# Gate/up products of a decoder layer: two matmuls instead of three, whole PSUM banks, copies on ScalarE, an accumulating DMA

## The chip, the cores and the metric

The kernel runs on one core of one Trainium2 chip. The metric is the device time of a run in microseconds (us); lower is better. Three runs of the kernel before gave 2072.7 us as median (2071.96 to 2073.09).

## What is computed

One layer of a decoder with 512 positions and model width 2048, everything in float32: a norm, an input projection, two kinds of windowed attention, an output projection, and then the feed-forward part that this document is about. Cut to that part, the reference reads:

```python
h = rmsnorm(x, ffn_norm[l])
gate = jnp.einsum('bsd,df->bsf', h, w_gate[l])     # 512 x 2048 by 2048 x 5632
up = jnp.einsum('bsd,df->bsf', h, w_up[l])         # the same shape
x = x + jnp.einsum('bsf,fd->bsd', jax.nn.silu(gate) * up, w_down[l])
```

## The kernel before

**Precision.** A float32 product is made out of the faster fp32r type. Each operand is split into a high part (a copy rounded to fp32r) and a low part (what is left), and three matmuls are added into PSUM: high times high, high times low, low times high. The function `three` (lines 437 to 441) issues them.

**Seven products instead of eight.** Gate and up form a block product of 2 by 2 blocks: two blocks of weights by two blocks of the 512 positions, over pairs of depth blocks. The kernel uses a fast scheme of Strassen's kind: seven products of sums of blocks, each with 128 weight columns and 256 positions (`HALF`), stand for eight plain ones. The sums of the position blocks are made once (`s_hi`, `s_lo`, seven slots of 256 for each of eight pairs). The sums of the weight blocks are made for each tile of weights.

**Groups and doubles.** The 5632 columns of gate and up are 44 groups (`TILES`) of 128 columns. A group goes over the depth in four steps, called doubles, so there are 176. In a double, the queue of SyncE (SP) loads the gate and the up weights (two DMAs, line 355) into one of three buffers `t_raw`; VectorE (DVE) makes the sums (`t_sums`, lines 1467 and 1470); ScalarE (ACT) makes the high parts (`t_high`, line 1012: 128x1792); VectorE makes the low parts (`t_low`, line 1476); TensorE (PE) runs `double` (lines 516 to 528): two depth blocks, seven products, three matmuls each with 256 moving columns, 42 in all. The step `t_high` of a double waits until TensorE is done with the double three before it, since there are three buffers.

**PSUM.** The seven 256-wide results share four banks (`PRODUCTS`, line 70), and groups alternate between two sets of four banks, so that a group accumulates while the one before it is read.

**After a group.** `cross` (lines 1015 to 1022) copies three of the results to SBUF on ScalarE. `post_first` and `post_second` (lines 1480 to 1497) combine the seven results into gate and up with four VectorE instructions that read PSUM. `store_gu` (lines 357 to 361) on SP's queue writes the 512 KB tile to DRAM (`gu_mid`), from two alternating buffers.

**Order.** Each engine's order is written out by hand. In `six_groups` VectorE runs `t_sums(j)`, then `t_low(j - 1)`; the combining of the group before comes in behind the latter where j % 4 is 3 (first half) and in the next step (second half). ScalarE runs `t_high(j)`, then `cross` where j % 4 is 2. GpSimd (POOL) does nothing in this stage but one small power.

**The next stage** is the down projection: 44 tiles of activation are loaded back, silu and the product are made, each is split into high and low (`down_high`, `down_low`), and TensorE runs units of twelve 512-wide matmuls (`down_unit`, lines 530 to 545, `wide_products`, lines 477 to 482).

Of the kernel before, what the change touches and what calls it, by code (L numbers as in the profile page):

```python
# [9 lines left out]
F32R = mybir.dt.float32r  # L10
# [60 lines left out]
BOTH, CROSS, OTHER, SPREAD = 0, 1, 2, 3  # L71
SPREAD_T = 27
# [15 lines left out]
def build(nc, x, attn_norm, w_in, sinks, out_norm_a, out_norm_b, w_out, ffn_norm,  # L88
# [90 lines left out]
    s_hi = [sb(f"s_hi{j}", [P, QUAD, HALF], F32R, at=places_s[j]) for j in range(KD // 2)]  # L179
    s_lo = [sb(f"s_lo{j}", [P, QUAD, HALF], F32R, at=places_s[j] + S_SIZE) for j in range(KD // 2)]  # L180
# [7 lines left out]
    gu_out = [sb(f"gu_out{r}", [P, 4, HALF], at=place_ez + 4096 * r) for r in range(2)]  # L188
    crossed = sb("crossed", [P, 3, HALF], at=place_ez + 8192)
    junk = sb("junk", [P, SEQ], at=place_ez + 9216)  # L190
    r2_bc = sb("r2_bc", [P, SEQ], at=place_x)
    r2_wide = sb("r2_wide", [P, NT, P], at=place_x + 6144)

    places_u = [place_x + 2048, place_raw0, place_raw0 + 4096, place_raw1, place_raw1 + 4096,
# [44 lines left out]
    crossed_done, post_done = sem("crossed_done"), sem("post_done")  # L239
    gu_stored = [sem(f"gu_stored{r}") for r in range(2)]  # L240
# [73 lines left out]
    def _(sp):  # L314
# [42 lines left out]
        def store_gu(i, gj):  # L357

            dst = gu_mid[bass.ds(LOOP_G * i + gj, 1), :, :].rearrange("o p c -> p (o c)")
            sp.wait_ge(post_done, 4 * (LOOP_G * i + gj) + 4)  # L360
            sp.dma_start(dst, gu_out[gj % 2][:, :, :].rearrange("p a c -> p (a c)")).then_inc(gu_stored[gj % 2], 16)

# [5 lines left out]
        with sp.Fori(0, 7) as i:  # L368
            for j in range(8, 32):
                load_double(i, j)  # L370
                if j % 4 == 2:
                    store_gu(i, j // 4 - 2)

        def load_gu(i, k):

            src = gu_mid[bass.ds(8 * i + k, 1), :, :].rearrange("o p c -> p (o c)")
            if isinstance(i, int) and i < 2:
                sp.wait_ge(gu_stored[k % 2], 16 * (4 * i + k // 2 + 1))
# [8 lines left out]

        load_gu(0, 0)
# [9 lines left out]
        store_gu(7, 0)  # L398
        for s in range(4, 32):
# [9 lines left out]
            if s == 15:  # L409
                store_gu(7, 1)  # L410
            if 16 <= s < 24:
                load_gu(1, s - 16)
        for r in range(2):
            sp.wait_ge(gu_stored[r], 16 * TILES // 2)
# [21 lines left out]
    def _(pe):  # L436
# [79 lines left out]
        def double(j):  # L516
# [3 lines left out]
            for q in range(2):  # L520
                sh, sl = s_hi[2 * d + q], s_lo[2 * d + q]
                for ti, si, which, h in PRODUCTS:
                    b = bank[BANK_SET[gj % 2][which]][:, HALF * h:HALF * (h + 1)]
                    if j == SPREAD_T + 1 and q == 0 and which == SPREAD:
                        pe.wait_ge(rbc_done, 2)
                    mm = three(b, t_hi[r][:, ti, q, :], t_lo[r][:, ti, q, :], sh[:, si, :], sl[:, si, :],
                               d == 0 and q == 0 and h == 0, d == DOUBLES - 1 and q == 1)
            mm.then_inc(t_used, 1)

        def down_unit(i, s):  # L530
# [6 lines left out]
            for t in range(NT):  # L537
                if k == 0 and isinstance(i, int) and i == 0 and n < 2:
                    pe.wait_ge(post_done, 4 * (TILES - 1 + n))
                elif k == 0:  # L540
                    pe.wait_ge(grp_taken, 4 * group + t - 7)
# [200 lines left out]
        for j in range(ALL_T):  # L742
# [5 lines left out]
            if g >= 2 and d == 0:  # L748
                pe.wait_ge(post_done, 4 * (g - 1))
            double(j)  # L750
            if j == 0:
                turn_mix(NC - 1)
            if j == SPREAD_T:
                pe.wait_ge(post_done, 4 * g)
                spread_r(r2_wide, 2, BANK_SET[(g + 1) % 2][SPREAD])
# [28 lines left out]
    def _(act):  # L784
# [230 lines left out]
        def cross(i, gj):  # L1015

            b = half_banks(gj, CROSS)
            act.wait_ge(t_used, used_by(i, gj))
            if not (isinstance(i, int) and i == 0 and gj == 0):
                act.wait_ge(post_done, 4 * (LOOP_G * i + gj) - 2)  # L1020
            nc.scalar.activation(crossed[:, 0:2, :], b, ACT.Copy).then_inc(crossed_done, 1)
            nc.scalar.activation(crossed[:, 2, :], b[:, 0, :], ACT.Copy).then_inc(crossed_done, 1)
# [785 lines left out]
```

## Time and profile before

| | |
|---|---|
| median of three runs | 2072.7 us |
| the profiled execution | 2072.31 us |
| its span, first to last instruction | 2070.5 us |
| granted TensorE clock, mean | 0.998 of full speed |
| TensorE (PE) busy | 2046.9 us (99%) |
| VectorE (DVE) busy | 1448.5 us (70%) |
| ScalarE (ACT) busy | 874.2 us (42%) |
| GpSimd (POOL) busy | 117.9 us (6%) |

The profile is of one execution. Matmuls are pipelined and the end of each is modelled, so the duration of a matmul says less than the distance from one start to the next. Busy time of an engine that waits for another is no cost; a wait matters where it sits on the chain that ends last.

### The profile page before, as it was taken

The page shows a single profiled execution, that of the slowest core. Times are in us where ns is not written, and L with a number is a line of the kernel's source. Part 1 is how long each engine was busy: PE and PEld are TensorE (multiplying, and loading weights), DVE is VectorE, ACT ScalarE, POOL GpSimd, SP SyncE. Part 2 cuts the span into 40 slices and gives each one's busy share as a digit, 9 for nine tenths or more (in the row PEclk, how much of TensorE's full clock was granted, in tenths as well). Part 3 has the DMA queues.
Part 4 walks back from the last instruction along what each step waited for, and adds up shares of the span by engine and source line. Part 5 has one row for each costly group of instructions (what it writes and reads, how often), then busy time and mean ns, then how long its engine had stood idle before and what let it go on. Part 6 is the DMA issues. An engine that isn't in the chain of part 4 may idle for free.

```text
span 2070.5 us, 35030 instructions
## 1 busy us (share of the span) xinstructions
PE 2046.9 (99%) x12886; PEld 1851.5 (89%) x12886; DVE 1448.5 (70%) x2174; ACT 874.2 (42%) x1381; POOL 117.9 (6%) x191
## 2 busy tenths in 40 slices
PE   8999999999999899999999999999999999999998
PEld 7888888887888899999999999999999888888886
DVE  5466666666666898787878888787887646545446
ACT  5455556555436533333333333333334333333333
POOL 0022222222100000000000000000000000000000
PEclk9999999999999999999999999999999999999999
DMA  6322222224334344444444444444447763654533
GB/s 188 92 71 78 72 73 73 72 71 152 78 99 139 112 143 126 138 132 126 134 131 134 123 136 133 129 133 129 136 123 233 249 178 97 177 138 136 137 96 132
DMA packets 317391, 261.41 MB, mean 126 GB/s; under 512 B 13872, under 2 KB 268128, under 8 KB 316768
## 3 DMA queue, kind: packets, MB, share of 16 engines
q1 hardware_dynamic: 309840, 248.11, 40.6%
q10 hardware_dynamic: 7440, 11.72, 1.6%
q8 instruction: 83, 1.36, 0.3%
q14 instruction: 28, 0.23, 0.0%
HBM read 228.31 MB, written 31.46 MB: 125 GB/s over the span
## 4 chain that ended last, share of the span: by engine, by line
PE 82%; DVE 6%; issue 5%; ACT 5%; DMA 1%; SPq 0%; ACTq 0%; DVEq 0%; POOLq 0%; POOL 0%
PE bank L439 18%; PE bank L441 18%; PE bank L440 18%; PE bank L480 9%; PE bank L482 9%; PE bank L481 9%; ACT probs L833 1%; PE bank L569 1%; ACT w_hi L790 1%; DVE w_lo L1195 1%; ACT s_raw L999 1%; DVE s_lo L1460 1%; PE bank L586 1%; PE bank L585 1%; ACT s_hi L982 1%
## 5 line engine op out<-in xcount | busy, mean ns | idle before, releaser
L439 PE MATMUL bank<-s_hi,t_hi 128*128 128x256 f32 x2464 | 698.5, 283 | 5.7 <-DVE t_lo L1476 5.7
L440 PE MATMUL bank<-s_lo,t_hi 128*128 128x256 f32 x2464 | 698.0, 283 | 0.0
L441 PE MATMUL bank<-s_hi,t_lo 128*128 128x256 f32 x2464 | 697.9, 283 | 0.0
L1012 ACT ACTIVATE t_hi<-t_raw 128x1792 fp32r<-128x1792 f32 x176 | 299.6, 1703 | 536.9 <-PE bank L441 509.0
L1195 DVE TENSOR_TENSOR w_lo<-raw,w_hi 128x512 fp32r<-128x512 f32 x364 | 253.2, 697 | 388.0 <-ACT w_hi L790 385.8
L439 PEld LDWEIGHTS bank<-s_hi,t_hi 128*128 128x128 f32 x2464 | 473.7, 192 | 6.6 <-issue 6.6
L440 PEld LDWEIGHTS bank<-s_lo,t_hi 128*128 128x128 f32 x2464 | 473.8, 192 | 0.0
L441 PEld LDWEIGHTS bank<-s_hi,t_lo 128*128 128x128 f32 x2464 | 473.8, 192 | 0.0
L1476 DVE TENSOR_TENSOR t_lo<-t_raw,t_hi 128x1792 fp32r<-128x1792 f32 x176 | 356.3, 2025 | 145.7 <-ACT t_hi L1012 145.7
L790 ACT ACTIVATE w_hi<-raw 128x512 fp32r<-128x512 f32 x364 | 229.1, 631 | 491.2 <-PE bank L482 355.1
L480 PE MATMUL bank<-w_hi,down_hi 128*128 128x512 f32 x640 | 249.0, 389 | 0.0
L481 PE MATMUL bank<-w_lo,down_hi 128*128 128x512 f32 x640 | 249.0, 389 | 0.0
L482 PE MATMUL bank<-w_hi,down_lo 128*128 128x512 f32 x640 | 249.0, 389 | 0.0
L1467 DVE TENSOR_TENSOR t_raw<-t_raw 128x1024 f32<-128x1024 f32 x176 | 214.3, 1217 | 7.0 <-DMA t_raw<-in_w_up 6.9
L439 PE MATMUL bank<-h_hi,w_hi 128*128 128x512 f32 x544 | 218.6, 402 | 0.4 <-DVE h_lo L1199 0.4
L441 PE MATMUL bank<-h_hi,w_lo 128*128 128x512 f32 x544 | 212.9, 391 | 0.0
L440 PE MATMUL bank<-h_lo,w_hi 128*128 128x512 f32 x544 | 212.8, 391 | 0.0
L482 PEld LDWEIGHTS bank<-w_hi,down_lo 128*128 128x128 f32 x640 | 120.1, 188 | 25.2
L480 PEld LDWEIGHTS bank<-w_hi,down_hi 128*128 128x128 f32 x640 | 120.1, 188 | 24.8
L481 PEld LDWEIGHTS bank<-w_lo,down_hi 128*128 128x128 f32 x640 | 120.1, 188 | 24.8
L441 PEld LDWEIGHTS bank<-h_hi,w_lo 128*128 128x128 f32 x544 | 102.1, 188 | 22.5
L439 PEld LDWEIGHTS bank<-h_hi,w_hi 128*128 128x128 f32 x544 | 102.4, 188 | 19.5 <-DVE h_lo L1199 0.8
(162 smaller groups left out, 2280.9 us busy)
## 6 DMA issues: line engine op xcount, KB each, us to landing
raw<-in_w_down SPq DMA_DIRECT2D x176, 256.0 KB, 2.9
t_raw<-in_w_gate SPq DMA_DIRECT2D x174, 256.0 KB, 3.1
t_raw<-in_w_up SPq DMA_DIRECT2D x174, 256.0 KB, 3.4
raw<-in_w_in SPq DMA_DIRECT2D x136, 256.0 KB, 2.9
gu_mid<-gu_out SPq DMA_DIRECT2D x44, 512.0 KB, 3.8
gu_s<-gu_mid SPq DMA_DIRECT2D x44, 512.0 KB, 5.1
raw<-in_w_out SPq DMA_DIRECT2D x64, 256.0 KB, 2.9
x_first<-in_x SPq DMA_DIRECT2D x8, 512.0 KB, 7.4
```

Of the source, the lines that this page charges most:

```text
L439: nc.tensor.matmul(out_ap, st_hi, mv_hi, start=start, stop=False, skip_group_check=True)
L440: nc.tensor.matmul(out_ap, st_hi, mv_lo, start=False, stop=False, skip_group_check=True)
L441: return nc.tensor.matmul(out_ap, st_lo, mv_hi, start=False, stop=stop, skip_group_check=True)
L480: nc.tensor.matmul(b[:, :], ah[:, ts], w_hi[:, slot, :], start=first, stop=False, skip_group_check=True)
L481: nc.tensor.matmul(b[:, :], ah[:, ts], w_lo[:, slot, :], start=False, stop=False, skip_group_check=True)
L482: return nc.tensor.matmul(b[:, :], al[:, ts], w_hi[:, slot, :], start=False, stop=last, skip_group_check=True)
L569: mm = nc.tensor.transpose(bank[BANK_PT][:, c0 + P * n:c0 + P * (n + 1)], probs[h % 2][:, e:e + P], ident[:, :])
L790: nc.scalar.activation(w_hi[:, s, :], raw[:, s, :], ACT.Copy).then_inc(w_hi_done, 1)
L1012: nc.scalar.activation(t_hi[r][:, :, :, :].rearrange("p a q c -> p (a q c)"), t_raw[r][:, 1:8, :, :].rearrange("p a q c -> p (a q c)"), AC ...
L1195: nc.vector.tensor_tensor(w_lo[:, s, :], raw[:, s, :], w_hi[:, s, :].bitcast(F32), ALU.subtract).then_inc(w_lo_done, 1)
L1467: nc.vector.tensor_tensor(x[:, 2:6, :].rearrange("p (a b) c -> p a b c", b=2), x[:, 0:9:8, :].unsqueeze(2).broadcast_to([P, 2, 2, HALF]), ...
L1476: nc.vector.tensor_tensor(t_lo[r][:, :, :, :].rearrange("p a q c -> p (a q c)"), t_raw[r][:, 1:8, :, :].rearrange("p a q c -> p (a q c)"), ...
```

## The change

For the groups from the third on (42 of 44):

- **Matmuls.** The high and low parts of the position sums become one tile (`s_two`, 2 by 7 by 256). High weights by both halves is one matmul of 512 moving columns; low weights by the high half is a second of 256. Two matmuls stand where three stood; the number of moving columns stays 768.
- **PSUM.** Each product takes a bank of its own (columns 0 to 255: the high positions; 256 to 511: the low positions). Seven banks are in use, and every group uses the same seven. The first double of a group waits, product by product, for the bank to have been copied out.
- **Copies.** ScalarE copies both halves of each of the seven banks to SBUF, 14 copies of 128x256 a group: the low halves into `part_low`, the high ones into `part`. It does so ahead of `t_high` where j % 4 is 2, and product by product as TensorE finishes them. There is one buffer of each.
- **Adding the halves.** GpSimd's queue issues a DMA (`fold`) from `part_low` to `part`, both in SBUF, 128 x 7168 bytes (896 KB), with add as accumulate operation.
- **Combining.** `post` on VectorE has five instructions, all on SBUF, in one place (behind `t_low(j - 1)` where j % 4 is 3), and first waits for the fold. The store to DRAM is issued by GpSimd's queue and waits for `post`. The next group's copies wait for the fold and `post` of the group before, and from the fourth product on for its store.
- The first two groups keep the three matmuls, but are copied out by ScalarE with four copies each (`take_halves`) and combined by `post`. Some small tiles move, and the last group's copies stand ahead of the second tile's high part in the down stage.

The core of the diff (places of tiles and the down stage are left out):

```diff
+SEVEN = [(0, 4, 4), (6, 3, 5), (5, 2, 6), (2, 5, 1), (3, 1, 2), (1, 6, 0), (4, 0, 3)]
+SEVEN_BANK = (0, 4, 6, 1, 2, 3, 5)
...
+    def taken_by(i, gj):
+
+        g = LOOP_G * i + gj
+        return 4 * (g + 1) if isinstance(g, int) and g < 2 else 14 * g - 6
...
+        def double_wide(j):
+
+            r, (g, d) = j % RING_T, (j // DOUBLES, j % DOUBLES)
+            pe.wait_ge(t_lo_done, j + 1)
+            for i, (ti, si, _) in enumerate(SEVEN):
+                b = bank[SEVEN_BANK[i]]
+                if d == 0 and g == 2:
+                    pe.wait_ge(bank_taken, 4 if i < 4 else i + 1)
+                elif d == 0:
+                    pe.wait_ge(bank_taken, taken_by(0, g - 2) + 2 * (i + 1))
+                for q in range(2):
+                    both = s_two[2 * d + q][:, :, si, :]
+                    nc.tensor.matmul(b[:, :].rearrange("p (a c) -> p a c", c=HALF), t_hi[r][:, ti, q, :], both,
+                                     start=d == 0 and q == 0, stop=False, skip_group_check=True)
+                    mm = nc.tensor.matmul(b[:, 0:HALF], t_lo[r][:, ti, q, :], both[:, 0, :], start=False,
+                                          stop=d == DOUBLES - 1 and q == 1, skip_group_check=True)
+                if d == DOUBLES - 1 and i < QUAD - 1:
+                    mm.then_inc(prod_ready, 1)
             mm.then_inc(t_used, 1)
...
+        def take_products(i, gj, i0=0, i1=QUAD):
+
+            g = LOOP_G * i + gj
+            for p in range(i0, i1):
+                b, slot = bank[SEVEN_BANK[p]], SEVEN[p][2]
+                if p == 0:
+                    slots_free(i, gj, False)
...
+                        act.wait_ge(folded, 16 * (g - 2))
+                if p == 3:
+                    slots_free(i, gj, True)
+                if p < QUAD - 1:
+                    act.wait_ge(prod_ready, (QUAD - 1) * (g - 2) + p + 1)
+                else:
+                    act.wait_ge(t_used, used_by(i, gj))
+                nc.scalar.activation(part_low[:, slot, :], b[:, HALF:2 * HALF], ACT.Copy).then_inc(bank_taken, 1)
+                nc.scalar.activation(part[:, slot, :], b[:, 0:HALF], ACT.Copy).then_inc(bank_taken, 1)
...
+                if j % 4 == 2 and not (first and j == 10):
+                    take_products(i, j // 4 - 1)
                 t_high(i, j)
                 if first and j == 8:
-                    cross(0, 0)
-                if j % 4 == 2:
-                    cross(i, j // 4 - 1)
+                    take_halves(0)
+                if first and j == 10:
+                    take_halves(1)
...
+        def post(i, gj):
+
+            g = LOOP_G * i + gj
+            if isinstance(g, int) and g < 2:
+                dve.wait_ge(bank_taken, taken_by(i, gj))
+            else:
+                dve.wait_ge(folded, 16 * (g - 1))
+            nc.vector.tensor_tensor(part[:, 1, :], part[:, 1, :], part[:, 5, :], ALU.add).then_inc(post_done, 1)
+            nc.vector.tensor_tensor(part[:, 2, :], part[:, 2, :], part[:, 4, :], ALU.add).then_inc(post_done, 1)
+            dve.wait_ge(post_done, POSTS * g + 2)
+            nc.vector.tensor_tensor(part[:, 1:3, :], part[:, 1:3, :], part[:, 0:4:3, :], ALU.add).then_inc(post_done, 1)
+            dve.wait_ge(post_done, POSTS * g + 3)
+            nc.vector.tensor_tensor(part[:, 1:3, :], part[:, 1:3, :], part[:, 6:7, :].broadcast_to([P, 2, HALF]), ALU.add).then_inc(post_done, 1)
+            nc.vector.tensor_tensor(part[:, 0:4:3, :], part[:, 0:4:3, :], part[:, 4:6, :], ALU.subtract).then_inc(post_done, 1)
...
                 if first and j == 8:
-                    post_first(0, 0)
-                if j % 4 == 0:
-                    post_second(i, j // 4 - 2)
+                    post(0, 0)
                 if j % 4 == 3:
-                    post_first(i, j // 4 - 1)
+                    post(i, j // 4 - 1)
...
+        def store_gu(g):
+
+            pool.wait_ge(post_done, POSTS * (g + 1))
+            nc.gpsimd.dma_start(gu_mid[g, :, :], part[:, 0:4, :].rearrange("p a c -> p (a c)")).then_inc(gu_stored, 16)
+
+        def fold(g):
+
+            pool.wait_ge(bank_taken, taken_by(0, g))
+            nc.gpsimd.dma_start(part[:, :, :].rearrange("p a c -> p (a c)"), part_low[:, :, :].rearrange("p a c -> p (a c)"),
+                                accum_op=ALU.add).then_inc(folded, 16)
+
+        for g in range(TILES):
+            if g >= 2:
+                fold(g)
+            store_gu(g)
```

## Rows read from the trace of the kernel before

**Rows 1.** The page: busy time of each engine, and the chain that ended last.

```profile
PE 2046.9 (99%) x12886; PEld 1851.5 (89%) x12886; DVE 1448.5 (70%) x2174; ACT 874.2 (42%) x1381; POOL 117.9 (6%) x191
PE 82%; DVE 6%; issue 5%; ACT 5%; DMA 1%; SPq 0%; ACTq 0%; DVEq 0%; POOLq 0%; POOL 0%
```

**Rows 2.** Stretches: busy us of PE, PEld, DVE, ACT, POOL; clock, DMA share, GB/s.

```profile
600.00:700.00 100.00, 96.21 (x478) 81.78 (x477) 64.75 (x82) 53.26 (x97) 0.00 (x0) 0.98 0.45 130
...
770.00:1400.00 630.00, 630.00 (x5253) 630.00 (x5252) 514.57 (x506) 236.84 (x188) 0.00 (x0) 1.00 0.43 131
```

**Rows 3.** Timeline of PE, gate/up stage: start us, duration us, engine, line, operation.

```profile
1199.78 0.28 PE L439 MATMUL bank<-s_hi,t_hi 128*128 128x256 f32 x1
1199.90 0.28 PE L440 MATMUL bank<-s_lo,t_hi 128*128 128x256 f32 x1
...
1201.94 0.28 PE L439 MATMUL bank<-s_hi,t_hi 128*128 128x256 f32 x1
```

**Rows 4.** Timeline of PE, down stage.

```profile
1700.21 0.39 PE L480 MATMUL bank<-w_hi,down_hi 128*128 128x512 f32 x1
...
1701.57 0.39 PE L480 MATMUL bank<-w_hi,down_hi 128*128 128x512 f32 x1
```

**Rows 5.** Timeline of ACT, gate/up stage; in brackets the idle time before, and its releaser.

```profile
1201.12 1.70 ACT L1012 ACTIVATE t_hi<-t_raw 128x1792 fp32r<-128x1792 f32 x1 [3.34 <-PE bank L441]
1202.73 0.57 ACT L1021 ACTIVATE crossed<-bank 128x512 f32<-128x512 f32 x1
1203.20 0.38 ACT L1022 ACTIVATE crossed<-bank 128x256 f32<-128x256 f32 x1
```

**Rows 6.** Timeline of DVE, gate/up stage: first its third group, then the middle.

```profile
749.45 1.21 DVE L1467 TENSOR_TENSOR t_raw<-t_raw 128x1024 f32<-128x1024 f32 x1
750.58 0.42 DVE L1470 TENSOR_TENSOR t_raw<-t_raw 128x256 f32<-128x256 f32 x1
750.92 2.02 DVE L1476 TENSOR_TENSOR t_lo<-t_raw,t_hi 128x1792 fp32r<-128x1792 f32 x1
752.85 1.22 DVE L1467 TENSOR_TENSOR t_raw<-t_raw 128x1024 f32<-128x1024 f32 x1
...
1202.86 2.02 DVE L1476 TENSOR_TENSOR t_lo<-t_raw,t_hi 128x1792 fp32r<-128x1792 f32 x1 [1.54 <-ACT t_hi L1012]
1204.80 0.68 DVE L1487 TENSOR_TENSOR gu_out<-bank,crossed 128x512 f32<-128x512 f32 x1
1205.40 0.68 DVE L1488 TENSOR_TENSOR gu_out<-bank,crossed 128x512 f32<-128x512 f32 x1
...
1209.84 0.69 DVE L1494 TENSOR_TENSOR gu_out<-bank,gu_out 128x512 f32<-128x512 f32 x1
1210.56 0.69 DVE L1496 TENSOR_TENSOR gu_out<-bank,gu_out 128x512 f32<-128x512 f32 x1
```

**Rows 7.** Waits in the stage, 740 to 1605 us: us in total, times, longest us.

```profile
ACT t_hi L1012 <- PE bank L441: 509.0, 162, 3.4
DVE t_lo L1476 <- ACT t_hi L1012: 143.3, 158, 2.9
```

**Rows 8.** DMA issues: out<-in, queue, count, KB each, median us to landing.

```profile
t_raw<-in_w_up SPq DMA_DIRECT2D x174, 256.0 KB, 3.4
gu_mid<-gu_out SPq DMA_DIRECT2D x44, 512.0 KB, 3.8
x_mix<-in_x ACTq DMA_DIRECT2D x4, 1024.0 KB, 10.3
x_mid<-x_mix ACTq DMA_DIRECT2D x4, 1024.0 KB, 4.5
out_x<-x_res SPq DMA_DIRECT2D x3, 1024.0 KB, 3.8
out_x<-x_res SPq DMA_DIRECT2D x1, 512.0 KB, 2.6
```

**Rows 9.** Start of the stage: PE's third group begins; ACT and DVE before it.

```profile
736.22 0.36 PE L439 MATMUL bank<-s_hi,t_hi 128*128 128x256 f32 x1 [0.23 <-DVE t_lo L1476]
...
728.99 0.58 ACT L1021 ACTIVATE crossed<-bank 128x512 f32<-128x512 f32 x1
...
729.93 0.69 DVE L1487 TENSOR_TENSOR gu_out<-bank,crossed 128x512 f32<-128x512 f32 x1 [0.66 <-ACT crossed L1022]
```

**Rows 10.** End of the stage: DVE's second low part; PE's first 512-wide matmuls of the down stage.

```profile
1581.53 0.68 DVE L1204 TENSOR_TENSOR down_lo<-gu_s,down_hi 128x512 fp32r<-128x512 f32 x1
...
L480 PE MATMUL bank<-w_hi,down_hi x24: 389/389/396, 1583.9 to 1599.6; 128*128 128x512 f32 x24
```

More of the change, by code:

```diff
@@ L187, in build @@
     t_lo = [sb(f"t_lo{r}", [P, QUAD, 2, P], F32R, at=places_t[r] + S_SIZE) for r in range(RING_T)]
-    gu_out = [sb(f"gu_out{r}", [P, 4, HALF], at=place_ez + 4096 * r) for r in range(2)]
-    crossed = sb("crossed", [P, 3, HALF], at=place_ez + 8192)
+    part = sb("part", [P, QUAD, HALF], at=place_ez)
+    part_low = sb("part_low", [P, QUAD, HALF], at=place_x)
     junk = sb("junk", [P, SEQ], at=place_ez + 9216)
-    r2_bc = sb("r2_bc", [P, SEQ], at=place_x)
-    r2_wide = sb("r2_wide", [P, NT, P], at=place_x + 6144)
-    places_u = [place_x + 2048, place_raw0, place_raw0 + 4096, place_raw1, place_raw1 + 4096,
+    junk_last = sb("junk_last", [P, SEQ], at=place_x)
+    r2_bc = sb("r2_bc", [P, SEQ], at=place_g + 14336)
+    r2_wide = sb("r2_wide", [P, NT, P], at=place_ez + 7168)
+    places_u = [place_ez + 7168, place_raw0, place_raw0 + 4096, place_raw1, place_raw1 + 4096,
                 place_t1, place_t1 + 4096, place_t1 + 8192]
@@ L747, in _ @@
                 pe.wait_ge(s_raw_done, 40)
-            if g >= 2 and d == 0:
-                pe.wait_ge(post_done, 4 * (g - 1))
-            double(j)
+            if g < 2:
+                double(j)
+            else:
+                double_wide(j)
             if j == 0:
@@ L1013, in t_high, with slots_free, take_halves @@
                                  t_raw[r][:, 1:8, :, :].rearrange("p a q c -> p (a q c)"), ACT.Copy).then_inc(t_hi_done, 1)
[L1015 to L1022, printed above, removed]
+        def slots_free(i, gj, stored_too):
+            g = LOOP_G * i + gj
+            act.wait_ge(post_done, POSTS * g)
+            if stored_too:
+                act.wait_ge(gu_stored, 16 * g)
+        def take_halves(gj):
+            act.wait_ge(t_used, used_by(0, gj))
+            if gj == 0:
+                act.wait_ge(s_sum_done, 3 * 8)
+            else:
+                slots_free(0, gj, True)
+            for which, slots in ((BOTH, slice(0, 4, 3)), (CROSS, slice(4, 6)), (OTHER, slice(1, 3)), (SPREAD, slice(6, 7))):
+                b = half_banks(gj, which)
+                if which == SPREAD:
+                    b = b[:, 0:1, :]
+                nc.scalar.activation(part[:, slots, :], b, ACT.Copy).then_inc(bank_taken, 1)
+        def take_products(i, gj, i0=0, i1=QUAD):
[4 more added lines that the diff above has]
+                    slots_free(i, gj, False)
+                    if isinstance(g, int) and g == 2:
+                        act.wait_ge(x_spilled[NC - 1], 16)
+                        act.wait_ge(sq_done, FIRST_SQ + 16)
+                    else:
+                        act.wait_ge(folded, 16 * (g - 2))
[3 more added lines that the diff above has]
+                    act.wait_ge(prod_ready, (QUAD - 1) * (g - 2) + p + 1)
+                else:
+                    act.wait_ge(t_used, used_by(i, gj))
+                nc.scalar.activation(part_low[:, slot, :], b[:, HALF:2 * HALF], ACT.Copy).then_inc(bank_taken, 1)
+                nc.scalar.activation(part[:, slot, :], b[:, 0:HALF], ACT.Copy).then_inc(bank_taken, 1)
         act.wait_ge(kb_lo_done, 4)
@@ L1138, in down @@
                     silu(0, s + 4)
-                if first and s == 6:
-                    cross(7, 1)
                 if 13 <= s < 13 + next_tiles:
@@ L1635, in down @@
                 if first and s == 6:
-                    post_first(7, 1)
-                    post_second(7, 1)
+                    post(7, 1)
                 if s % 8 < 2:
@@ L1649, in down @@
                     down_low(i + 1, s - 25)
-        for k in range(2):
-            gate_scaled(0, k)
+        gate_scaled(0, 0)
         gate_times_up(0, 0)
```

85 lines of the change are left out of this document (34 added, 51 removed).

## The prediction

> **What bounds the kernel now.** I read the page first: TensorE is busy for 99% of the span and makes up 82% of the chain that ended last [rows 1]. Then the stretch of the gate/up stage, from 770 us on: in 630 us TensorE never pauses, at full clock, while VectorE works 514.6 us, ScalarE 236.8 us, GpSimd nothing, and the DMA engines 43% [rows 2]. Then the starts of its matmuls. From 1199.78 to 1201.94 us there are 18 steps of 0.120 us [rows 3], for 256 columns each. In the down stage 6 steps of 512 columns take 1.36 us, 0.2267 us each [rows 4]. The difference, 256 columns in 0.1067 us, is 2.4 GHz exactly. So each matmul costs 0.1067 us per 256 columns **and a further 0.0133 us**, whether it is wide or narrow. A double of 42 narrow matmuls takes 5.04 us, a group of four 20.15 us.
>
> Last I read who waits. ScalarE's high parts wait for TensorE to free a buffer (509 us in all) and VectorE's low parts for ScalarE (143 us) [rows 7]. Both engines run ahead: at 1201.12 ScalarE begins the high parts of a double, VectorE has the low ones at 1204.8 [rows 5, 6], and TensorE wants them two doubles (10.1 us) after the buffer came free. About 6 us of slack.
>
> **The matmuls.** In 42 groups x 4 doubles x 14 triples = 2352 places, three matmuls (0.360 us) become one of 512 and one of 256: 0.2267 + 0.120 = 0.3467 us. That is 0.0133 us each, 31 us in all; a group falls from 20.15 to 19.41 us. No row has a 512-wide matmul whose moving columns lie in two pieces; from below I bound it by the row of a contiguous one (no cost), from above by two narrow ones, which would give back all 31 us. The row it is nearest to is the contiguous one; I take that. If two pieces cost as much as two matmuls, nothing is gained.
>
> The Trainium skill, "TensorE: Matmul & The Clock Gate", section "Wait — 56ns, not 53.3ns?", gives about 2.5 ns as the fixed cost of a warm matmul. By it the change would be worth 6 us. Rows 3 and 4 show 13.3 ns for this kernel's fp32r matmuls, and the sum goes by them.
>
> **ScalarE.** Out go two copies a group (0.57 and 0.38 us), in come 14 of 128x256. Back to back a copy costs its duration less 0.10 us (1202.73 to 1203.20 for one of 0.57) [rows 5], so 0.28 us, 3.9 us a group. With four high parts at 1.61 us that is 10.3 us of 19.4: room enough. They are hidden in part by the last double of a group: ScalarE is free 2.1 us into it, TensorE finishes a product every 0.69 us and the copies need 0.56, so they end about 1.1 us after the group. The first double of the next group asks for its banks in the same order, 0.69 us apart from the group's end on; the bank asked for last is wanted 4.2 us after it. Cost of the seven banks: nothing, 3 us of cover.
>
> **VectorE.** A double is 1.47 us of sums and 1.93 us of low parts, start to start [rows 6]. Four instructions of 2.6 us a group go. The five of post: two of 256 wide (0.36 and 0.48), one of 512 behind a wait (0.75), two more of 0.60 to 0.65 (from the distances 0.60 and 0.72 in rows 6): 2.8 us. Together 16.4 of 19.4 us. Enough, if VectorE isn't made to wait.
>
> **SP's queue** loses 44 issues of stores; nothing waits for them. GpSimd's queue gets 44 stores and 42 folds and has nothing else. Its store is needed only at the fourth product of the next group's copies; 3.8 us [rows 8] or twice that fits.
>
> **The fold and what is queued behind it** decide the case. Post waits in order on VectorE until the fold has landed, and behind post stand the sums of one double and the low parts of another that TensorE needs. Call L the time from the last copy to the moment VectorE sees the fold. If the fold is late, the group becomes a loop: post 2.8, sums 1.47, low 1.93, sums of the next double 1.47 (0.1 to be seen), high parts 1.61, 14 copies 3.86 (0.15 to be seen), and L again: **13.4 + L**. Up to L = 6.0 us TensorE's 19.41 stays the longer; at L = 6.7 the group is as long as before; from there each us of L costs 42 us.
>
> No row has an accumulating DMA or one issued by GpSimd. Bounds: from below the 1024 KB store without other traffic, 3.8 us; from above the 1024 KB load beside other traffic, 10.3 us. The nearest row is the store of 1024 KB from SBUF beside weight loads, 4.5 us [rows 8]: nearly the same size, the same source, and a DMA share of 0.45 around it against 0.43 in the stage [rows 2]. For issue by software and the second operand I add 1 us, an estimate between the ends: L = 5.5. So the fold stays hidden, with half a us of cover only.
>
> **Ends of the stage.** At its start there is no slack: TensorE waits 0.23 us for low parts at 736.22 [rows 9]. VectorE's combining waits for ScalarE there, whose copies of the first group now take 1.9 us instead of 0.9, +1.1 us; the second group's copies stand behind a high part, and the new group's fifth product waits for them, some 0.8 us. I take 2 us (0 to 5). At the end, the second tile's low part was ready at 1582.2, 4 us before it was wanted [rows 10]; the first unit begins at about 1583.5 and has 12 matmuls of 0.2267 us. The last group's copies now stand ahead of it; by the same chain it comes 0.4 us before it is wanted. I take 0.5 us (0 to 3).
>
> **Sum**, against the profiled execution's own 2072.3 us (the median of the runs is 2072.7, 0.4 above it): -31.0 + 2.0 + 0.5 = **2043.8 us**.
>
> **Rivals.**
> (a) *The accumulating DMA moves its data at half speed.* It must read part_low and part and write part. By rows 8, 512 and 1024 KB without traffic take 2.6 and 3.8 us: 1.2 us for 512 KB over a fixed 1.4. A second read of 896 KB adds 2.1 us to the 4.5 of the nearest row: L = 6.6, group 20.0 us, time 2072.3 - 42 x 0.15 + 2.5 = 2068.5. The stage's own stores speak for traffic that counts (3.8 us against 2.6).
> The Trainium skill, "Collectives: The Full Stack", section "The bandwidth ceiling: the fold count and why AG ≠ RS ≠ AR", states such a rule: an add in the DMA path needs two reads that share one ring, and so runs at about half the rate of a copy. No row here can show it.
> (b) *Slower.* The same, plus 1 us or so for GpSimd's issue and the second read stretched by the weight loads, which arrive every 4.9 us: L = 7.5, group 20.9, and the loop through VectorE's queue, not TensorE, sets the pace. 2072.3 + 42 x 0.75 + 2.5 = 2106. With L = 8, 2127; at the upper bound of 10.3, 2224. It decides from L = 6.8 on. For it: the cover is thin, both buffers are single, and no row excludes it. Against it: the store at 4.5 us.
> (c) *The wide matmul in two pieces brings nothing*: 20.15 a group, 2075 at best, about no change.
>
> **Chances.** Forecast (L up to 6.0) 0.43. Partly used up (6.0 to 6.6, the case of (a)) 0.11, 2044 to 2068. Within 0.2%, about 4 us, which is what a measurement of this kernel can tell from no change: 0.06, from (a) at its far end and (c). (b) 0.40. So faster 0.54, same 0.06, slower 0.40. The forecast's own range is 2041 to 2049; since both signs hold much of the chance, the range for 8 in 10 runs from 2040 to L = 8.1, 2130.
>
> **What the profile after would show.** Right: starts of a wide and a narrow matmul 0.347 us apart for the pair; a group of 19.4 us; TensorE without idle time in the stage; VectorE waiting for the fold before post but the low parts still early; fold to landing under 6 us. Wrong: TensorE idle once a group ahead of its fourth double, released by t_lo, and VectorE idle ahead of post, released by the DMA; then L can be read from the landing and the loop's sum checked. If the pair takes 0.36 us, it is (c). If TensorE is idle ahead of a group's first double, the banks are late, which I have priced at nothing.

## The result, and the profile of the kernel after

The change makes the kernel slower. Four runs gave a median of 2152.3 us (2151.9 to 2154.1), against 2072.9 us for four runs of the kernel before: a ratio of 1.0385, interval 1.0371 to 1.0400, or 79.5 us. The profiled execution took 2152.76 us, its span 2150.8 us, at a mean clock of 0.989.

The page: busy time, then the chain that ended last, by engine and by line.

```profile
PE 2053.3 (95%) x10534; PEld 1737.2 (81%) x10534; DVE 1449.9 (67%) x2218; ACT 1004.7 (47%) x1889; POOL 178.9 (8%) x277
...
PE 47%; DVE 17%; DMA 16%; issue 9%; ACT 9%; ACTq 0%; SPq 0%; DVEq 0%; POOL 0%; POOLq 0%
DMA part<-part_low 16%; PE bank L480 9%; PE bank L482 9%; PE bank L481 9%; DVE t_lo L1530 4%; PE bank L439 4%; PE bank L441 4%; PE bank L440 4%; PE bank L540 4%; DVE t_raw L1521 3%; ACT part L1075 3%; ACT part_low L1074 2%; PE bank L542 2%; DVE part L1544 1%; ACT w_hi L811 1%
```

Against [rows 1] TensorE's share of the chain falls from 82% to 47%, and one DMA, the fold, holds 16%. A share like that for a transfer that was to be hidden is the first thing to see. There are 2352 matmuls fewer, as written, so the change does what it says.

The same stretch as in [rows 2], and the four us of it in which the clock was low:

```profile
770.00:1400.00 630.00, 581.57 (x3207) 499.57 (x3206) 475.59 (x496) 305.46 (x522) 39.84 (x57) 0.98 0.62 161
1196.00:1200.00 4.00, 4.00 (x17) 3.44 (x17) 3.35 (x4) 2.80 (x6) 0.00 (x0) 0.64 0.44 131
```

TensorE now stands still for 48 of 630 us, where it never paused before. VectorE's busy time in the whole span didn't grow (1449.9 against 1448.5 us; the 630 us hold fewer groups now), nor is any other engine near its limit. So nothing is too busy: something is waited for in turn. The waits of 700 to 1700 us say what (line, releaser: us in total, times, longest):

```profile
ACT t_hi L1033 <- DVE t_raw L1524: 383.7, 89, 8.7
DVE part L1541 <- DMA part<-part_low: 179.9, 41, 6.7
ACT t_hi L1033 <- PE bank L542: 88.1, 40, 8.1
...
PE bank L540 <- DVE t_lo L1530: 67.2, 42, 2.7
DVE t_raw L1521 <- DMA t_raw<-in_w_up: 40.3, 47, 1.9
...
PE bank L540 <- ACT part L1075: 1.3, 1, 1.3
```

Read them from the bottom up. The banks, which I had priced at nothing, cost 1.3 us once. TensorE waits once a group for low parts, 67 us in all. ScalarE's high parts used to wait for TensorE [rows 7]; now they wait for VectorE's sums. And VectorE waits 4.4 us in each group, at the first instruction of `post`, for the fold. The DMA issues (KB each, median us from issue to landing) give its length, against a neighbour and the store:

```profile
t_raw<-in_w_up SPq DMA_DIRECT2D x174, 256.0 KB, 4.0
part<-part_low POOLq DMA_DIRECT2D x42, 896.0 KB, 8.1
gu_mid<-part POOLq DMA_DIRECT2D x44, 512.0 KB, 2.9
```

One turn of the loop, from the timelines of VectorE, ScalarE, GpSimd and TensorE (start us, duration, what it is, idle time before and its releaser):

```profile
1211.52 0.43 DVE L1541 TENSOR_TENSOR part<-part 128x256 f32<-128x256 f32 x1 [4.70 <-DMA part<-part_low]
...
1213.65 0.68 DVE L1547 TENSOR_TENSOR part<-part 128x512 f32<-128x512 f32 x1
1214.25 1.22 DVE L1521 TENSOR_TENSOR t_raw<-t_raw 128x1024 f32<-128x1024 f32 x1
...
1215.72 2.02 DVE L1530 TENSOR_TENSOR t_lo<-t_raw,t_hi 128x1792 fp32r<-128x1792 f32 x1
1217.66 1.22 DVE L1521 TENSOR_TENSOR t_raw<-t_raw 128x1024 f32<-128x1024 f32 x1
...
1217.79 0.50 PE L540 MATMUL bank<-s_two,t_hi 128*128 128x512 f32 x1 [0.48 <-DVE t_lo L1530]
...
1219.24 1.71 ACT L1033 ACTIVATE t_hi<-t_raw 128x1792 fp32r<-128x1792 f32 x1 [1.70 <-DVE t_raw L1524]
...
1224.27 0.54 ACT L1075 ACTIVATE part<-bank 128x256 f32<-128x256 f32 x1
...
1225.11 0.85 POOL L1817 DMA_DIRECT2D part<-part_low  x1 [9.93 <-ACT part L1075]
...
1232.91 0.42 DVE L1541 TENSOR_TENSOR part<-part 128x256 f32<-128x256 f32 x1 [3.72 <-DMA part<-part_low]
```

From `post` to `post` 21.39 us: 13.29 us until the last copy ends at 1224.81 (post, sums, low parts, sums, high parts, 14 copies, the loop of the prediction), and 8.10 us more until VectorE sees the fold. TensorE isn't in this loop at all; it is fed late by it. Over 40 such turns in the timeline, the loop without the fold has a median of 13.30 us, and L, the time from the last copy to the first instruction of `post`, a median of 8.4 and a mean of 8.45.

**The sum of the slowdown.** The mean over the 40 groups is 22.01 us against 20.15 before: 74.4 us. Of it (13.30 + 8.45 - 20.15) x 40 = 64 us are the loop, and 10 us are excesses over 13.30, nearly all in eleven groups, which the last section takes up under the clock. The remaining 6 us of the difference of the two spans (80.3) lie at the ends of the stage.

### The profile page after: what moved, and what is told of

It is laid out like the page before. It is cut to its first block, busy times and chain, and to the rows that moved or that the text cites. A ratio compares the mean times of both kernels' runs of the same rounds, so it can differ in the third digit from the quotient of the medians.

```text
span 2150.8 us, 31007 instructions
## 1 busy us (share of the span) xinstructions
PE 2053.3 (95%) x10534; PEld 1737.2 (81%) x10534; DVE 1449.9 (67%) x2218; ACT 1004.7 (47%) x1889; POOL 178.9 (8%) x277
## 4 chain that ended last, share of the span: by engine, by line
PE 47%; DVE 17%; DMA 16%; issue 9%; ACT 9%; ACTq 0%; SPq 0%; DVEq 0%; POOL 0%; POOLq 0%
DMA part<-part_low 16%; PE bank L480 9%; PE bank L482 9%; PE bank L481 9%; DVE t_lo L1530 4%; PE bank L439 4%; PE bank L441 4%; PE bank L440 4%; PE bank L540 4%; DVE t_raw L1521 3%; ACT part L1075 3%; ACT part_low L1074 2%; PE bank L542 2%; DVE part L1544 1%; ACT w_hi L811 1%
## 5 line engine op out<-in xcount | busy, mean ns | idle before, releaser
L540 PE MATMUL bank<-s_two,t_hi 128*128 128x512 f32 x2352 | 847.6, 404 | 69.1 <-DVE t_lo L1530 67.2
L542 PE MATMUL bank<-s_two,t_lo 128*128 128x256 f32 x2352 | 666.5, 283 | 0.0
L540 PEld LDWEIGHTS bank<-s_two,t_hi 128*128 128x128 f32 x2352 | 450.2, 191 | 189.1 <-DVE t_lo L1530 81.9
L1033 ACT ACTIVATE t_hi<-t_raw 128x1792 fp32r<-128x1792 f32 x176 | 304.0, 1728 | 482.0 <-DVE t_raw L1524 393.8
L542 PEld LDWEIGHTS bank<-s_two,t_lo 128*128 128x128 f32 x2352 | 452.8, 193 | 0.0
L1521 DVE TENSOR_TENSOR t_raw<-t_raw 128x1024 f32<-128x1024 f32 x176 | 214.8, 1220 | 40.5 <-DMA t_raw<-in_w_up 40.3
L1541 DVE TENSOR_TENSOR part<-part 128x256 f32<-128x256 f32 x44 | 18.7, 425 | 181.5 <-DMA part<-part_low 179.9
L1075 ACT ACTIVATE part<-bank 128x256 f32<-128x256 f32 x294 | 128.7, 438 | 0.0
L1074 ACT ACTIVATE part_low<-bank 128x256 f32<-128x256 f32 x294 | 125.6, 427 | 1.9 <-PE bank L542 1.0
```

The costliest lines, as they stand in the source:

```text
L540: nc.tensor.matmul(b[:, :].rearrange("p (a c) -> p a c", c=HALF), t_hi[r][:, ti, q, :], both, start=d == 0 and q == 0, stop=False, skip_gr ...
L542: mm = nc.tensor.matmul(b[:, 0:HALF], t_lo[r][:, ti, q, :], both[:, 0, :], start=False, stop=d == DOUBLES - 1 and q == 1, skip_group_check ...
L1033: nc.scalar.activation(t_hi[r][:, :, :, :].rearrange("p a q c -> p (a q c)"), t_raw[r][:, 1:8, :, :].rearrange("p a q c -> p (a q c)"), AC ...
L1521: nc.vector.tensor_tensor(x[:, 2:6, :].rearrange("p (a b) c -> p a b c", b=2), x[:, 0:9:8, :].unsqueeze(2).broadcast_to([P, 2, 2, HALF]), ...
```

## Experiments

The first three kernels below and the one without a fold were run once each, the others four to ten times. Each is compared with the kernel before, run beside it. Two explanations were to be told apart at first: that the adding in the DMA makes it slow, or that the transfer as such, its issue by GpSimd or its company of weight loads, does. And one question stood beside them: does anything but the fold cost time?

**The fold as a plain copy.** All else is kept, the same bytes go to the same place, but they overwrite the high halves there: the two halves aren't added.

```diff
-            nc.gpsimd.dma_start(part[...], part_low[...], accum_op=ALU.add).then_inc(folded, 16)
+            nc.gpsimd.dma_start(part[...], part_low[...]).then_inc(folded, 16)
```

> The fold is a plain copy from part_low to part (no adding, so the two halves are not added). Theory A (the accumulating DMA moves its packets one by one at less than half the rate of a copy, and that is most of the late fold): by the 4096-byte packets of the store, 896 KB need about 2.3 us of data phase instead of 4.6, the time L from the last copy to the start of post falls from 8.4 to about 6.0 us, the loop through VectorE's queue (13.3 + L) to 19.3 us, so that TensorE's 14 pairs x 4 doubles x 0.350 = 19.6 us is the longer; time about 2055 us. Theory B (issue by GpSimd and the traffic of the weight loads are what makes it late, the adding costs nothing): L stays at 7.5 to 8.4, time 2110 to 2152 us.

Measured: 2059.1 us, beside 2073.1 for the kernel before on that chip. L falls to 5.5 us and the group to 19.8 us. That is more than the loop needs (13.3 + 5.5 = 18.8 us): TensorE sets the pace here, at a distance of its matmuls that the section "VectorE adds, no fold" explains. The DMA view of one fold in each kernel (queue, kind: packets, MB, share of 16 engines; then the issues), first after, in 1225 to 1233 us:

```profile
q0 software_dynamic: 144, 0.92, 71.0%
...
part<-part_low POOLq DMA_DIRECT2D x1, 896.0 KB, 7.8
t_raw<-in_w_gate SPq DMA_DIRECT2D x2, 256.0 KB, 7.0
t_raw<-in_w_up SPq DMA_DIRECT2D x2, 256.0 KB, 7.4
```

and the plain copy, 1211 to 1220 us:

```profile
q0 software_dynamic: 144, 0.92, 24.3%
...
part<-part_low POOLq DMA_DIRECT2D x1, 896.0 KB, 5.7
t_raw<-in_w_gate SPq DMA_DIRECT2D x2, 256.0 KB, 3.1
t_raw<-in_w_up SPq DMA_DIRECT2D x2, 256.0 KB, 3.5
```

The same 0.92 MB occupies the 16 engines for 0.71 x 8 = 5.7 us when it is added, for 0.243 x 9 = 2.2 us when it is copied. Over the whole stage the median packet of 7168 bytes takes 553 ns against 273 ns, and each engine has eight of them. The loads issued beside it land in 7.0 to 7.4 us in place of 3.1 to 3.5. GpSimd also spends 0.86 us on each issue of the adding DMA and 0.53 us on one of the plain. So it is the adding. The Trainium skill, "Collectives: The Full Stack", section "The bandwidth ceiling: the fold count and why AG ≠ RS ≠ AR", gives a reason for a collective that adds (ReduceScatter): two operands are read through one ring, at about half the rate of a copy. The trace agrees with the rate, with a factor of 2.0 for the median packet; that one ring is the cause, no run here shows. The estimate for a plain transfer of this size by the Trainium skill, "DMA: Bandwidth & Descriptors", section "Anatomy of one DMA — SWDGE (gpsimd) path", is about 4.1 us; 5.1 us were measured as the median here, with weight loads on the same engines, and 4.2 us where `post` stands later (below).

**The plain copy issued by ScalarE.** The copy stands in ScalarE's queue behind the last of the fourteen, GpSimd issues only the stores.

```diff
+            if i1 == QUAD:
+                act.wait_ge(bank_taken, taken_by(i, gj))
+                act.dma_start(part[...], part_low[...]).then_inc(folded, 16)
```

> The same plain copy (the halves are not added), issued by ScalarE's queue right behind its last copy instead of by GpSimd. It measures what the issue by GpSimd adds to L. Theory A: about 1 us, L about 5.0, time about 2055 us as in the kernel with the plain copy from GpSimd, since both are below the 6.3 us from which TensorE waits. Theory B: most of L is the issue by GpSimd, so L falls from 7.5 or more to 5 or less and the time from over 2110 to 2055 us.

Measured: 2063.5 us, L 5.5 us, median landing 5.5 us where GpSimd's was 5.1. Issue by GpSimd costs nothing that shows in L, and the us that I had put between the two queues isn't there. The 4.4 us by which this kernel is the slower of the two fit TensorE's matmuls, whose pairs keep the longer of two distances throughout here and in some 60% of the stage there (see "VectorE adds, no fold").

**Three of seven slots added.** The fold moves 384 KB and still adds; the low halves of the other four slots are left out.

```diff
-            nc.gpsimd.dma_start(part[:, :, :]..., part_low[:, :, :]..., accum_op=ALU.add)
+            nc.gpsimd.dma_start(part[:, 4:7, :]..., part_low[:, 4:7, :]..., accum_op=ALU.add)
```

> The accumulating DMA takes three of the seven slots (384 KB instead of 896 KB; the low halves of the other four are not added). Theory A: the data phase is 3/7 of 4.6 us, 2.0 us, so L is about 5.8 us and TensorE doesn't wait; time about 2055 us. Theory B (fixed costs of the software queue): L falls by less than 1 us, time over 2100 us.

Measured: 2050.8 us, L 5.7 us, landing 5.4, a group of 19.44 us. With 3/7 of the bytes L falls by 2.7 of 8.4 us. From these two points I estimate a part of L that goes with bytes, about 2.7 us for 512 KB, and a fixed one of some 3.7 us. Below 6 us it is hidden, as the prediction had it.

**No fold.** The low halves are copied out but never added. `post` waits for the copies in place of the fold, and the next group's copies no longer wait for a fold.

```diff
-                dve.wait_ge(folded, 16 * (g - 1))
+            dve.wait_ge(bank_taken, taken_by(i, gj))
```

> No fold at all (the low halves are copied out but not added); post waits for the copies. It shows what the change gives without its DMA: 31 us less for the matmuls, 3 to 5 us for the two ends of the stage: 2045 to 2049 us, and TensorE's pairs at 0.347 us as in the kernel that adds three slots. If the pairs stay at 0.350 us or the time is over 2060 us, something other than the fold holds the stage up too.

Measured: 2047.0 us beside 2073.8, so 26.8 us faster. The group takes 19.41 us from `post` to `post`, the number of the prediction; past the start of the stage TensorE waits but once, 1.3 us for a bank. Six steps from wide matmul to wide matmul take 2.08 us, 0.3467 each:

```profile
1203.80 0.39 PE L540 MATMUL bank<-s_two,t_hi 128*128 128x512 f32 x1
1204.03 0.28 PE L542 MATMUL bank<-s_two,t_lo 128*128 128x256 f32 x1
...
1205.88 0.39 PE L540 MATMUL bank<-s_two,t_hi 128*128 128x512 f32 x1
```

This settles three points at once: the wide matmul in two pieces costs no more than a contiguous one; seven single banks and 14 copies cost 1.3 us; and all but some 4 us of the 31 arrive. Whatever the change loses, it loses by the fold.

**The fold in two.** Slots 4 to 6, whose banks are copied first, are folded while ScalarE copies the other four.

```diff
+            for taken, slots in ((taken_by(0, g) - 8, slice(4, 7)), (taken_by(0, g), slice(0, 4))):
+                pool.wait_ge(bank_taken, taken)
+                nc.gpsimd.dma_start(part[:, slots, :]..., part_low[:, slots, :]..., accum_op=ALU.add).then_inc(folded, 16)
```

> The fold is two accumulating DMAs: slots 4 to 6 as soon as the first three products are copied out, slots 0 to 3 (512 KB) behind the last copy; post where the changed kernel has it, output the reference's. Theory A: what counts is the data phase of what is left after the last copy, 4/7 of 4.7 us, 2.7 us, so L is 6.0 to 6.4 us instead of 8.4, the loop (13.3 + L) 19.3 to 19.7 us, about TensorE's own 19.5; time 2050 to 2060 us, faster than both kernels. If the two DMAs share the engines so that the first holds up the second, L stays over 7.5 and the time over 2105 us.

Measured: 2080.3 us, ratio 1.0031 (1.0019 to 1.0044): no faster than before. L is 6.7 us, more than expected, and the period 20.07 us. The loop without the fold again takes 13.29 us in the median: the loop's sum holds at a second value of L. The second piece takes 6.4 us for 512 KB, more than the 5.4 that 384 KB took alone.

**`post` one double later.** Nothing is made shorter; `post` goes behind the low parts of the next double, so the fold has one double more before VectorE's queue stands behind it.

```diff
-                if j % 4 == 3:
-                    post(i, j // 4 - 1)
+                if j % 4 == 0:
+                    post(i, j // 4 - 2)
```

> Post stands one step later in VectorE's order, behind the low parts of the next double (where j % 4 is 0), everything else as in the changed kernel, output the reference's. Theory A (the loss is the work queued behind the waiting post): L stays at about 8.4 us, but the low parts that TensorE wants for its fourth double are done before post waits; TensorE doesn't wait, a group takes 14 x 4 x 0.350 = 19.6 us, time 2072.9 - 42 x 0.55 + 5 = about 2055 us (2048 to 2065), and the dips of TensorE's clock go with the pauses. Rival C (the single buffer is the limit: fold, post, store and the next copies one behind another): the copies of the next group wait for the store or for post, time over 2100 us.

Measured: 2060.7 us as the median of ten runs between 2051.3 and 2084.7; the ratio, without the longest, is 0.9933 (0.9909 to 0.9958). In the middle of its runs, moving `post` turns 3.9% slower into 0.7% faster, with a fold about as long as before (7.8 us to landing, against 8.1); only 10 of the 42 `post` behind a fold wait for it. But the runs scatter as those of no other kernel here, and the profiled one took 2080.9 us. In its steady groups the period is 19.79; in others it is 21 to 23. One of these, from the timelines of GpSimd, SP and VectorE:

```profile
903.96 0.86 POOL L1816 DMA_DIRECT2D part<-part_low  x1 [6.52 <-ACT part L1075]
...
904.05 0.86 SPq L366 DMA_DIRECT2D t_raw<-in_w_up  x1
...
912.71 1.23 DVE L1521 TENSOR_TENSOR t_raw<-t_raw 128x1024 f32<-128x1024 f32 x1 [4.84 <-DMA t_raw<-in_w_up]
```

A weight load issued 0.09 us after the fold is seen 8.7 us later, where its median in the kernel after is 4.0. So when VectorE no longer waits for the fold, it may wait for the load that shares the engines with it. In the kernel after, such loads were late too, but VectorE stood still for the fold anyway. The steady 19.79 us aren't 19.41 because of the second distance of the matmuls (see "VectorE adds, no fold"); how much of the scatter comes from it and how much from late loads isn't shown.

**Both: in two, and later.**

> Both: the fold in two, and post one step later in VectorE's order; output the reference's. If the disturbed groups of the kernel with post later (weight loads that land 5 us late while the fold of 896 KB is in flight) come from the long fold, the shorter pieces end them: 2048 to 2056 us with little scatter. If they come from the place of post, the scatter of 2051 to 2085 us stays.

Measured: 2100.8 us, ratio 1.0132 (1.0117 to 1.0148), some 45 us above what was expected. The two edits, each a gain, don't add up. The waits of its stage, 740 to 1605 us:

```profile
DVE t_raw L1521 <- DMA t_raw<-in_w_up: 154.0, 78, 5.2
...
PE bank L540 <- ACT part L1075: 32.3, 29, 1.5
DVE part L1541 <- DMA part<-part_low: 4.5, 2, 3.9
```

The fold is hidden (4.5 us in all), and the loads are late instead (154 us, against 35 after in the same stretch). Which coincidence of loads and folds makes the period 21.0 us was not taken further.

**`post` later, and the plain copy.** The halves aren't added here either.

> Post one step later as before, and the fold a plain copy (the halves are not added). If the accumulating DMA's long packets are what made some weight loads 5 us late and the time scatter from 2051 to 2085 us, the scatter goes: all runs within 5 us, 2050 to 2062 us. If the later place of post does it (the store and the next fold move onto the loads), the scatter stays.

Measured: 2050.3 us in the median of four runs, three of them within 1 us and one at 2064.9; ratio 0.9911 (0.9882 to 0.9941). Against the kernel before that is 22.8 us faster, where the kernel without a fold was 26.8, and VectorE's longest wait for a weight load is 1.5 us, where it was 5.9 with the adding. It is the adding that disturbs the loads, not the place of `post`. All four within 5 us, as expected, they were not: the run of 2064.9 us has no trace, and what made it longer is open.

**GpSimd adds in SBUF.** The fold becomes a `tensor_tensor` of 128x1792 on GpSimd.

```diff
+            nc.gpsimd.tensor_tensor(part[:, :, :], part[:, :, :], part_low[:, :, :], ALU.add).then_inc(folded, 1)
```

> GpSimd adds the halves with one instruction of 128x1792 in place of the accumulating DMA; all else and the output as in the changed kernel. By its additions of 128x512 in the attention stage (1.3 us each) it needs 4.6 us, so L is about 4.9 us, under the 6.1 us from which TensorE waits. Theory A (only the lateness of the fold and its DMA traffic cost): no DMA traffic either, group 19.41 us as without a fold, time 2045 to 2050 us. Rival D (GpSimd and VectorE, both reading two operands from SBUF, slow each other): L over 6.5 us or VectorE's low parts longer than 2.02 us, time over 2065 us.

Measured: 2121.7 us, ratio 1.0235 (1.0219 to 1.0250). The timelines of GpSimd and VectorE:

```profile
1202.29 1.23 DVE L1521 TENSOR_TENSOR t_raw<-t_raw 128x1024 f32<-128x1024 f32 x1 [1.38 <-DMA t_raw<-in_w_up]
...
1204.66 5.04 POOL L1817 TENSOR_TENSOR part<-part,part_low 128x1792 f32<-128x1792 f32 x1 [9.70 <-ACT part L1075]
...
1205.70 5.08 DVE L1521 TENSOR_TENSOR t_raw<-t_raw 128x1024 f32<-128x1024 f32 x1
```

The addition is shorter than the DMA's 8.1 us, but the sums that VectorE runs beside it take 5.08 us in place of 1.23: they end at 1210.78, 1.08 us after GpSimd's addition does at 1209.70. The Trainium skill, "SBUF — State Buffer", section "SBUF: two separate sides", says that a GpSimd operation that reads SBUF and a VectorE one with two SBUF inputs take one pair of ports as an exclusive lock, and the later one fully blocks; the trace agrees.

**The same in three pieces**, each as soon as its banks are copied.

> The same additions in three pieces (slots 4 to 6 after the third product, 1 and 2 after the fifth, 0 and 3 after the last), so that 1.3 us of addition is left after the last copy: L 1.5 to 2.5 us. Theory A: TensorE is the bound in both, so no faster than the kernel with one addition: 2045 to 2050 us. Rival D: slower than the one with one addition where the additions collide with VectorE's low parts.

Measured: 2118.0 us, ratio 1.0217 (1.0204 to 1.0231). The standstill is spread (over the whole kernel, low parts take 2261 ns in the mean and sums 1467, against 2018 and 1220 with the plain copy) and not removed: an addition in pieces still stops VectorE for as long as it runs.

**VectorE adds, no fold.** ScalarE copies only the low halves (seven copies a group); VectorE adds each to the high half, which it reads in PSUM. No DMA, no fold.

```diff
+                dve.wait_ge(bank_taken, 7 * g - 6 + p + 1)
+                nc.vector.tensor_tensor(part[:, slot, :], bank[SEVEN_BANK[p]][:, 0:HALF], part_low[:, slot, :], ALU.add).then_inc(folded, 1)
```

> No fold and no DMA for it: ScalarE copies the low halves alone (7 copies a group), and VectorE adds each to the high half in PSUM as it comes (7 additions of 128x256, where j % 4 is 2), releasing the bank. Post as in the changed kernel; output the reference's. VectorE then has 13.6 + 2.8 + 7 x 0.36 = 18.9 us of work in a group of 19.4. Theory A (the wide matmuls are worth 31 us, what was lost was lost to the fold): TensorE stays the bound at 19.41 us a group, the ends of the stage cost 4 to 7 us, time 2046 to 2052 us. Rival E (VectorE is too full): TensorE waits for low parts, group 19.6 to 20.2 us, time 2056 to 2080 us.

Measured: 2060.1 us, ratio 0.9932 (0.9919 to 0.9946). VectorE is busy 596 of 630 us, and has room for it: TensorE's waits come to 5.8 us. The rest of the gain stays away for another reason: in some stretches a wide and a narrow matmul take 0.3533 us a pair, in others 0.3467. In the same place as above, six pairs take 2.12 us and not 2.08:

```profile
1203.80 0.40 PE L540 MATMUL bank<-s_two,t_hi 128*128 128x512 f32 x1
1204.05 0.28 PE L542 MATMUL bank<-s_two,t_lo 128*128 128x256 f32 x1
...
1205.92 0.40 PE L540 MATMUL bank<-s_two,t_hi 128*128 128x512 f32 x1
```

A group of 56 pairs takes 19.79 us at the one and 19.41 us at the other. This accounts for much of what set the kernels above apart. The plain copy from ScalarE keeps 0.3533 us for the whole stage and the one from GpSimd for some 60% of it (2063.5 and 2059.1 us); with three slots, without a fold, and with the plain copy and `post` later, most or all pairs take 0.3467 us (2050.8, 2047.0 and 2050.3 us). Six pairs of the plain copy from ScalarE, 2.12 us:

```profile
1203.70 0.40 PE L540 MATMUL bank<-s_two,t_hi 128*128 128x512 f32 x1
...
1205.82 0.40 PE L540 MATMUL bank<-s_two,t_hi 128*128 128x512 f32 x1
```

**Wide, wide, narrow, narrow.** As the last, but both wide matmuls of a product come before both narrow ones.

```diff
-                for q in range(2):
-                    (wide matmul q, narrow matmul q)
+                for q in range(2):
+                    (wide matmul q)
+                for q in range(2):
+                    (narrow matmul q)
```

> As the kernel in which VectorE adds the halves, but each product's four matmuls in a double are issued wide, wide, narrow, narrow instead of wide, narrow, wide, narrow; output the reference's. In the traces so far a pair of wide and narrow keeps one of two steady distances, 0.3467 or 0.3533 us, and changes between them only at a pause of TensorE; over 2352 pairs that is 16 us. If the alternation makes the second distance possible, two pairs take 0.693 us throughout and the time is 2045 to 2052 us with little scatter. If it is there in any mixture of widths, the time stays at 2055 to 2063 us.

Measured: 2056.8 us between 2055.9 and 2058.1, ratio 0.9920 (0.9906 to 0.9934). Two pairs take 0.697 us throughout, so 0.348 each, and there is no second distance: less scatter, and a mean between the two. It is neither what was expected of the one theory (0.693 us and 2045 to 2052) nor of the other (two distances). Three products, six pairs, take 2.09 us:

```profile
1203.77 0.63 PE L539 MATMUL bank<-s_two,t_hi 128*128 128x512 f32 x2
1204.24 0.39 PE L542 MATMUL bank<-s_two,t_lo 128*128 128x256 f32 x2
...
1205.86 0.40 PE L539 MATMUL bank<-s_two,t_hi 128*128 128x512 f32 x1
```

Of the kernels that compute the whole layer and repeat well it has the lowest time, 17 us below the kernel before and 96 below the one after; from the last one it isn't clearly told apart (ratios 0.9920 and 0.9932, with overlapping intervals). `post` later had runs down to 2051 us, but no steady ones.

## Why the prediction was wrong

The forecast of 2043.8 us was missed by 109 us; 104 of them are 40 groups of 22.01 us in place of 19.41. The step that failed is L, the time until VectorE sees the fold: 5.5 us in the forecast, 8.4 measured.

- **The matmuls** (-31.0 us): right. 19.41 us a group without the fold, and 26.8 us faster as a whole, where the forecast had 28.5. The measured 13.3 ns per matmul was the one to go by, not the 2.5 ns of the Trainium skill, "TensorE: Matmul & The Clock Gate", section "Wait — 56ns, not 53.3ns?": by that, 6 us would have been gained. The second steady distance of a pair (up to 16 us over 2352 pairs) I didn't foresee; it isn't in the trace of before, whose matmuls in this stage all have one width.
- **ScalarE's copies, seven banks, SP's and GpSimd's queues** (nothing): right, with 1.3 us of waits for banks.
- **The loop through VectorE's queue**, 13.4 + L: right to 0.1 us, at L = 8.4 (13.30) and at L = 6.7 (13.29). TensorE idle once a group ahead of its fourth double, released by `t_lo`, was the sign of being wrong that I had named. With the measured mean of L, 8.45, the prediction's own formula gives 2072.3 + 42 x (13.4 + 8.45 - 20.15) + 2.5 = 2146.2; 2152.8 was profiled.
- **L**: this is the step that failed. I took 5.5 us: 4.5 from the store of 1024 KB, and 1 us for issue by software and the second operand together. A plain copy takes just those 5.5 us, with none of it due to the queue; that the figure fits a copy is luck. The second operand, which I had folded into that one us, is worth 2.9 us by itself. Rival (a) had its mechanism and gave it 2.1 us on top of 4.5, without a fixed cost of its own: 6.6. Its price by bytes, 1.2 us for 512 KB, was low too: 2.7 us is the estimate from the two sizes that were added. Rival (b) had the sign and the structure; its L of 7.5 to 8 was still short.
- **The range** ended at L = 8.1, 2130 us (2131.5 by its own formula). The two terms that a trace of before could not show (half rate, and the time under weight loads) were each put at a middle value, though they lengthen the same transfer and therefore come together. The upper bound of the rows, 10.3 us or 2224 us, was the end to take for a cost with no row of its own, and the slope of 42 us per us of L was known. The forecast sat on the one flat part of that curve with half a us of cover.
- **Ends of the stage** (2.5 us): somewhat small. TensorE waits 1.13 and 0.60 us at the start and 2.24 + 0.55 + 0.17 us where the down stage begins, 4.7 in all, released as forecast but larger at the end, where the kernel without a fold waits 0.17 us:

```profile
738.21 0.50 PE L540 MATMUL bank<-s_two,t_hi 128*128 128x512 f32 x1 [1.13 <-DVE t_lo L1530]
741.90 0.50 PE L540 MATMUL bank<-s_two,t_hi 128*128 128x512 f32 x1 [0.60 <-ACT part L1054]
...
1661.13 0.47 PE L480 MATMUL bank<-w_hi,down_hi 128*128 128x512 f32 x1 [0.55 <-ACT part L1075]
1666.37 0.47 PE L480 MATMUL bank<-w_hi,down_hi 128*128 128x512 f32 x1 [2.24 <-DVE down_lo L1258]
```

## What to carry to other kernels

A DMA that adds in place isn't a copy with a free addition: price the second read, and the transfers beside it, before you put it behind a wait in an in-order queue. Where a new wait closes a loop, write the loop as a constant plus the unknown, find the value at which it takes the lead, and let the range reach as far as the unknown's bounds do, since beyond that point every us is paid once per turn. And where the wait can't be shortened, try moving the waiting instructions by one step first: it was a small edit here, and in the median worth more than splitting the transfer; then look at what is late next.

## What the runs showed of the hardware

- **An accumulating DMA from SBUF to SBUF** takes 8.1 us from issue to landing for 896 KB beside weight loads, and 5.4 us for 384 KB; a plain one takes 5.1 us for 896 KB. Others on the same engines are held up beside it: the loads of 256 KB issued beside one fold landed in 7.0 to 7.4 us, beside a plain copy in 3.1 to 3.5 (over all loads of the up weights the medians are 4.0 and 3.5).
- **Wide and narrow matmuls in turn keep one of two distances**, 0.3467 or 0.3533 us a pair, for long stretches. In most kernels it changed only at pauses of TensorE, but not in all, other than the last expectation says: where VectorE adds, it changed at about 979.8 and 1375.9 us with no pause there. What sets it is open.
- **The clock.** In the kernel after, TensorE's granted clock falls to half (1.2 GHz) eleven times in the stage, ten times for 3.4 us and once for 6.8; in the kernel before it never does there. The row of 1196 to 1200 us above holds one, in the double that began at 1195.75 after a pause of 1.80 us. Ten begin within 1.5 us behind a pause of 1.8 to 2.5 us, the long one inside a pause of 2.7 us (until 1501.67), but pauses of 2.36 us (until 1327.55) and 2.08 us (until 1084.90) have none behind them. They fall into the same eleven groups in which the loop took at least 0.3 us more than 13.30: nine by 0.4 us, the one with the long fall by 1.6, and one by 5.1, in which ScalarE also waits 4.5 us to copy the norm's scales. TensorE at half clock for 3.4 us does 1.7 us less work, and only a quarter of that is paid, since it isn't what sets the pace.
- **GpSimd and VectorE**: an addition of 128x1792 on GpSimd (4.5 us in the mean) stops one of 128x1024 on VectorE until it is done: 5.08 us in place of 1.22.
